# Reciprocal roots of the norms and of the last read-outs: ScalarE's logarithm and exponential with one Newton step, in place of an integer seed with three

## What is computed

```python
def rmsnorm(x, gain=None):
    xf = x.astype(jnp.float32)
    y = xf * lax.rsqrt(jnp.mean(xf * xf, axis=-1, keepdims=True) + EPS)
    ...

for l in range(DEPTH):
    hx = rmsnorm(x) * (1 + sc_a) + sh_a
    ...
    x = x + g_a * (jnp.concatenate([fx, ax, rx], axis=-1) @ w_out[l])
    x = x + g_f * swiglu(rmsnorm(x) * (1 + sc_f) + sh_f, w_gate[l], w_up[l], w_down[l])
return rmsnorm(x, final_norm)
```

## Time and profile before

| | |
|---|---|
| time, three runs | 1946.1 us median (1939.06, 1946.1, 1947.41) |
| span of the profiled execution | 1944.5 us |
| PE busy | 1773.0 us (91% of the span) |
| DVE busy | 1292.1 us (66%) |
| ACT busy | 839.4 us (43%), 12 loads of a table set among it |
| POOL busy | 83.8 us (4%) |
| DMA | 300.36 MB, mean 154 GB/s |

### The profile page before, as it was taken

The page is one execution under the profiler, slowest core; times in us unless marked ns, Lnnn a source line. Parts: engine busy times, 40 slices in busy tenths (PEclk is TensorE's granted clock), DMA queues, the critical chain, the costliest instruction groups (busy, mean ns, idle before and its releaser), DMA issues.

```text
span 1944.5 us, 30955 instructions
## 1 busy us (share of the span) xinstructions
PE 1773.0 (91%) x12242; PEld 1589.2 (82%) x12242; DVE 1292.1 (66%) x2365; ACT 839.4 (43%) x1661; POOL 83.8 (4%) x154
## 2 busy tenths in 40 slices
PE   4899988989999999898788999989899998989997
PEld 2788866888888888688678999777799987879996
DVE  1336678558878666557885788868678885675544
ACT  2523674252222222444653544366544435665432
POOL 1000124000000000001030000000000000000000
PEclk8889998899999999899787999989999998999999
DMA  8552111055546664234243899633399863416653
GB/s 252 184 190 87 33 45 45 6 150 170 173 162 204 186 189 160 85 111 114 84 135 84 255 263 281 237 120 78 109 264 274 274 228 113 127 44 174 184 175 130
DMA packets 359391, 300.36 MB, mean 154 GB/s; under 512 B 8320, under 2 KB 333680, under 8 KB 358992
## 3 DMA queue, kind: packets, MB, share of 16 engines
q1 hardware_dynamic: 357824, 294.22, 49.7%
q0 software_dynamic: 1424, 4.16, 0.9%
HBM read 297.30 MB, written 1.05 MB: 153 GB/s over the span
## 4 chain that ended last, share of the span: by engine, by line
PE 72%; DVE 11%; DMA 7%; ACT 5%; issue 4%; SPq 0%; DVEq 0%; POOL 0%; ACTq 0%; POOLq 0%
PE bank L958 70%; PE bank L972 2%; DMA raw<-in_w_up 2%; ACT whigh L1556 2%; DMA raw<-in_w_down 2%; DVE wlow L2057 1%; DVE ACC L2073 1%; DVE A L2430 1%; DMA A<-in_w_ada 1%; DMA raw<-in_ffn_w_out 1%; ACT A L1784 1%; DVE HTL L2182 1%; DMA X<-in_ctx 1%; DMA raw<-in_ffn_w_in 0%; DVE A L2174 0%
## 5 line engine op out<-in xcount | busy, mean ns | idle before, releaser
L2057 DVE TENSOR_TENSOR wlow<-raw,whigh 128x2048 fp32r<-128x2048 f32 (+1 forms) x183 | 409.8, 2243 | 301.5 <-ACT whigh L1556 301.0
L1556 ACT ACTIVATE whigh<-raw 128x2048 fp32r<-128x2048 f32 (+1 forms) x183 | 343.0, 1878 | 315.9 <-PE bank L958 99.1
L958 PE MATMUL bank<-HTH,whigh 128*128 128x256 f32 (+1 forms) x1424 | 444.4, 312 | 8.5 <-DVE HTL L2182 8.2
L958 PE MATMUL bank<-HTH,wlow 128*128 128x256 f32 (+1 forms) x1424 | 440.4, 309 | 0.0
L958 PE MATMUL bank<-HTL,whigh 128*128 128x256 f32 (+1 forms) x1424 | 440.2, 309 | 0.0
L958 PE MATMUL bank<-whigh,HTH 128*128 128x256 f32 (+1 forms) x1008 | 297.5, 295 | 23.0 <-DVE HTL L2300 6.3
L958 PE MATMUL bank<-wlow,HTH 128*128 128x256 f32 (+1 forms) x1008 | 293.1, 291 | 0.0
L958 PE MATMUL bank<-whigh,HTL 128*128 128x256 f32 (+1 forms) x1008 | 292.7, 290 | 0.0
L958 PEld LDWEIGHTS bank<-HTH,whigh 128*128 128x128 f32 x1424 | 273.6, 192 | 21.8 <-issue 8.9
L958 PEld LDWEIGHTS bank<-HTH,wlow 128*128 128x128 f32 x1424 | 273.4, 192 | 13.7
L958 PEld LDWEIGHTS bank<-HTL,whigh 128*128 128x128 f32 x1424 | 273.7, 192 | 12.6
(11 more groups left out here) (233 smaller groups left out, 2251.4 us busy)
## 6 DMA issues: line engine op xcount, KB each, us to landing
raw<-in_ffn_w_in SPq DMA_DIRECT2D x88, 512.0 KB, 5.4
A<-in_ada_w SPq DMA_DIRECT2D x38, 1024.0 KB, 7.4
A<-in_w_ada SPq DMA_DIRECT2D x32, 1024.0 KB, 5.5
raw<-in_w_gate SPq DMA_DIRECT2D x44, 512.0 KB, 6.6
raw<-in_w_up SPq DMA_DIRECT2D x44, 512.0 KB, 6.3
raw<-in_ffn_w_out SPq DMA_DIRECT2D x20, 1024.0 KB, 5.5
raw<-in_w_in SPq DMA_DIRECT2D x18, 1024.0 KB, 5.6
raw<-in_w_down SPq DMA_DIRECT2D x18, 1024.0 KB, 6.7
```

What stands on the lines that cost most here:

```text
L958: return nc.tensor.matmul(out, lhsT, rhs, start=start, stop=stop, skip_group_check=True)
L1556: nc.scalar.activation(parts(loads[n])[0], raw_slot(loads[n]), ACT.Copy).then_inc(*made("split_high", loads[n]))
L2057: V.tensor_tensor(low, raw_slot(loads[n]), as_float(high), ALU.subtract).then_inc(*made("split_low", loads[n]))
```

## The change

The integer guess and two of the three Newton steps are replaced, in ten places: the seven norms, the last norm, and the read-outs of tiles 0 and 1 in layers 0 and 1. There ScalarE computes Ln of the mean square and then Exp of minus half of it into `rs`, and VectorE, which meanwhile makes minus half the mean square, runs one Newton step on that (`polish`). In the norms ScalarE takes the mean inside the Ln: scale 1/D, and as bias the mean of the first half, column by column, one Ln per tile; then one Exp for all. These stand in ScalarE's list behind the squares of the second half and ahead of `norm_scaled(l, st, 0, 2, 3)`. In the norm before layer 2, and in the two read-outs, ScalarE waits for VectorE's mean square and runs one Ln and one Exp. `refine` stays for the first norm, the heads, the read-out of tiles 2 and 3, and `final_roots`. The preload of the set with Ln and Exp moves from the projections of layers 2 and 3 to the end of each layer's hidden features (behind `high(fs[-1])`, ahead of the down projection), in all four layers.

```diff
+            def root_seeds(l, st, tiles):
+                n = len(tiles)
+                if (l, st) == (2, "mix"):
+                    act.wait_ge(*upto("mean_square", l, st))
+                    last = nc.scalar.activation(logs[:, 0:n], ms[:, 0:n], ACT.Ln)
+                else:
+                    act.wait_ge(*upto("mean_half", l, st))
+                    for t in tiles:
+                        act.wait_ge(*upto("squared", l, st, 1, t))
+                        last = nc.scalar.activation(logs[:, t:t + 1], lsum[:, 1, t:t + 1], ACT.Ln, scale=1.0 / D, bias=ms[:, 8 + t:9 + t])
+                last.then_inc(*made("root_log", l, st))
+                act.wait_ge(*upto("root_log", l, st))
+                nc.scalar.activation(rs[:, 0:n], logs[:, 0:n], ACT.Exp, scale=-0.5).then_inc(*made("root_seed", l, st))
+
+            def head_seeds(l, t0, n):
+                act.wait_ge(*upto("mean_square", l, "scan", t0))
+                nc.scalar.activation(logs[:, 0:n], ms[:, 0:n], ACT.Ln).then_inc(*made("root_log", l, "scan"))
+                act.wait_ge(*upto("root_log", l, "scan"))
+                nc.scalar.activation(rs[:, 0:n], logs[:, 0:n], ACT.Exp, scale=-0.5).then_inc(*made("root_seed", l, "scan"))
...
             def norm(l, st):
                 tiles, more = tiles_of(l, st), len(pairs_of(l, st)) > 1
                 squares(l, st, tiles, lambda: norm_scaled(l, st, 0, 0, 1))
+                root_seeds(l, st, tiles)
                 norm_scaled(l, st, 0, 2, 3)
...
-                    if l >= 2 and at == 1:
-                        nc.scalar.preload_act_table_set("natural_log_exp_and_others")
...
                     high(fs[-1])
+                    if half == halves(l) - 1:
+                        nc.scalar.preload_act_table_set("natural_log_exp_and_others")
...
                         fourier_out(l, g)
+                        if g == 0:
+                            head_seeds(l, 0, 8)
...
                     squares(l, "final", X_TILES)
+                    root_seeds(l, "final", X_TILES)
...
+            def polish(l, st, n, done):
+                m, half, root, t = ms[:, 0:n], half_ms[:, 0:n], rs[:, 0:n], nw[:, 0:n]
+                link(V.tensor_scalar(half, m, -0.5, None, ALU.mult))
+                dve.wait_ge(*upto("root_seed", l, st))
+                link(V.tensor_tensor(t, root, root, ALU.mult))
+                link(V.tensor_tensor(t, t, half, ALU.mult))
+                V.scalar_tensor_tensor(out=root, in0=t, scalar=1.5, in1=root, op0=ALU.add, op1=ALU.mult).then_inc(*made(*done))
+
             def row_norms(l, st, tiles, done=None):
                 n = len(tiles)
+                if done:
+                    dve.wait_ge(*upto("squared", l, st, 0, tiles[-1]))
+                    V.tensor_scalar(ms[:, 8:8 + n], lsum[:, 0, 0:n], 1.0 / D, EPS, ALU.mult, ALU.add).then_inc(*made("mean_half", l, st))
+                    dve.wait_ge(*upto("squared", l, st, 1, tiles[-1]))
+                    dve.wait_ge(*upto("mean_half", l, st))
+                    link(V.scalar_tensor_tensor(out=ms[:, 0:n], in0=lsum[:, 1, 0:n], scalar=1.0 / D, in1=ms[:, 8:8 + n],
+                                                op0=ALU.mult, op1=ALU.add))
+                    polish(l, st, n, done)
+                    return
...
-                refine(2, "mix", n=2, done=("rooted", 2, "mix"))
+                dve.wait_ge(*upto("mean_square", 2, "mix"))
+                polish(2, "mix", 2, ("rooted", 2, "mix"))
...
-                refine(l, "scan", t0, n=4 * n)
+                if t0 == 0:
+                    dve.wait_ge(*upto("mean_square", l, "scan", t0))
+                    polish(l, "scan", 4 * n, ("rooted", l, "scan"))
+                    dve.wait_ge(*upto("rooted", l, "scan"))
+                else:
+                    refine(l, "scan", t0, n=4 * n)
```

More of the change, by code:

```diff
@@ L445, in block_kernel @@
         nw = sb("nw", [P, 16])
+        logs = sb("logs", [P, 8])
         nmax = sb("nmax", [P, 2, 4])
@@ L2701, in _ @@
                 if l == 3:
-                    row_norms(l, "final", X_TILES)
+                    row_norms(l, "final", X_TILES, ("rooted", l, "final"))
+                    dve.wait_ge(*upto("rooted", l, "final"))
                     dve.wait_ge(*upto("final_gain_in", l))
```

## The result

| kernel | median us | executions | profiled execution: time, span, clock |
|---|---|---|---|
| before | 1946.76 (1939.06 to 1949.46) | 4 | span 1944.5, clock 0.945 |
| after | 1929.38 (1926.24 to 1932.7) | 4 | 1932.7, span 1930.9, clock 0.956 |

The ratio after to before is 0.9919, with a 95% interval of 0.989 to 0.9947: 17.4 us between the medians, where 6.3 had been forecast and the range ended at 1932. The first question is how much of this lies at the roots.

A forecast was written before the change was run, and what follows sets the result against it. TensorE bounds the kernel, idle for the root chain in seven norms. 2 × 0.93 + 2 × 1.19 + 1.00 + 0.47 + 0.57 = 6.3 us; 1946.1 − 6.3 = 1939.8 us, range 1932 to 1946.

The forecast's parts named there:

- What bounds the kernel: At seven norms TensorE waits for the last Newton step; the whole root chain is on the path, the rest follows.
- The chain, term by term: Root chain in the norms: summed instruction times and hand-overs gave gains of 1.19 us with two tiles, 0.93 with four.
- T: In a norm, the end of the accumulator's last read; TensorE's spread started at T + 2.56 us before the change.
- Layer 2's mixing norm: Norm before layer 2, where ScalarE waits for VectorE's mean square: spread at 1283.59 in place of 1284.59, gain 1.00 us.
- These two norms give 0.47 and 0.57: Norms at 1073.68 and 1615.36: a 1.81 us gate row fills TensorE's time, capping gains at its idle 0.47 and 0.57.
- The hidden edits: Later ScalarE copies, the last norm, two read-outs and thirteen table loads in place of twelve: each 0 on the path.
- how the numbers follow: Closing step that set chances: 1939 to 1942 us 0.56, faster by over 0.5% 0.25, slower 0.04, within 0.71.
- the runs' own spread of 8 us: Spread of the kernel's run times, used with most of rival A and Rival B to set the range 1932 to 1946.
- rival A: Behind the norms: shorter stalls save TensorE stretches at half clock, 3 to 7 us more, 1933 to 1937; chance 0.22.
- if the clock's low stretches differ by more than two: A sign in the profile after that would make the prediction wrong: over two stretches of low clock more or fewer.
- Rival B: Feed-forward parts of layers 1 and 2: weight DMA waits absorb the gains up to layer 2, 1942.6 to 1944.3; chance 0.18.
- Rival C: In the norms: Ln or Exp from another table set brings two 1.28 us loads each, 1956.6 us; chance 0.04.

The follow-up runs named there:

- norms_only: The changed kernel with the two read-outs back on the integer guess and three Newton steps; median 1933.55 us, ratio to before 0.9969.
- pad_first12: The changed kernel with twelve extra dependent VectorE instructions in layer 0's feed-forward norm alone; median 1936.95 us, ratio to before 0.9968.
- pad_norms: The changed kernel with six extra dependent VectorE instructions in each of the seven norms; median 1938.45 us, ratio to before 1.0002.
- one_step: The kernel before with one Newton step instead of three behind the integer guess in the change's ten places; median 1930.67 us, ratio to before 0.9944.
- half_roots: The changed kernel with the squares of the second half of the columns left out in six norms; median 1922.71 us, ratio to before 0.9904.
- tables_in_norms: The changed kernel with the Ln and Exp table preload back in the projections of layers 2 and 3; median 1944.16 us, ratio to before 0.9987.
- pad_norms24: The changed kernel with 24 extra dependent VectorE instructions in each of the seven norms; median 1969.69 us, ratio to before 1.0144.
- after_third: The changed kernel run a third time, unaltered, in 11 executions; median 1938.74 us, ratio to before 0.9974.
- preload_only: The kernel before with only the Ln and Exp table preload moved to the end of the hidden features; median 1946.28 us, ratio to before 1.0029.
- before_early_gain: The kernel before with the final gain fetched early into the free half of its buffer; median 1942.37 us, ratio to before 1.0.
- early_gain: The changed kernel with the final gain fetched early into the free half of its buffer; median 1936.65 us, ratio to before 0.9953.

## Why the prediction was wrong

**What bounds the kernel: right.** Only TensorE's seven waits counted, and everything behind them followed at a fixed distance. Over the kernels, most of what the norms gain in the traces comes out in the time at equal clock: −7.0 and −7.0 (norms_only), −6.0 and −4.4 (pad_first12), +0.4 and −0.3 (pad_norms), −8.4 and −6.8 (one_step), −16.0 and −13.5 (half_roots), −7.6 and −6.4 ± 0.6 (the changed kernel, all executions). It does not for two: −0.35 and −3.5 (tables_in_norms), +27.5 and +15.6 (pad_norms24). There the plain means agree with the traces: −1.7 ± 1.7 and +27.2 ± 2.1 against before beside them.

**The chain, term by term: right in its mechanism.** Two tiles: spread at T + 1.31 where 1.37 was forecast, gain 1.25 for 1.19; the dependent start on ScalarE was 0.03 and not 0.09. Four tiles: T + 1.69 where 1.64 was forecast, because the Lns stand 0.19 apart and not 0.15. Layer 2's mixing norm: 1.11 for 1.00.

**"These two norms give 0.47 and 0.57": mis-sized.** Measured were 1.24, 1.25 and 0.60 for the first and 0.86, 1.25 and 1.02 for the second. The bound itself, the gate row that fills the time, is real: where that row ran at half clock, the first norm gave 0.60 (after_third) and 0.68 (norms_only). The row in after_third:

```profile
1071.77 1.91 PE L959 MATMUL bank<-ident,modc 128*128 128x128 f32 x8
```

But I took the row's 1.81 as fixed, and it is 1.06 at full clock. The sums came out 1.2, 1.6 and 1.1 us above 6.3, and these two norms make 1.1, 1.5 and 0.6 of that; in after_third another 0.5 is layer 2's mixing norm, whose gain was 1.49.

**The hidden edits: right.** The moved copies, the last norm (VectorE idle 2.54, forecast 2.4), the read-outs (norms_only, 7.0 without them) cost and gave nothing that can be told. Thirteen table loads, none in a norm. For the loads alone preload_only leaves room for about 1 us of loss.

**The step that failed is how the numbers follow, in two places.** First, the range: "the runs' own spread of 8 us" was read from three executions. The 86 executions of before that ran beside the experiments lie between 1930.4 and 1953.6, a spread of 23 us and not 8, with nine in ten between 1932.3 and 1951.3. Medians of four drawn from them lie between 1936.5 and 1949.2 in 95 of 100 cases, and of four drawn from the changed kernel's 21 between 1928.9 and 1941.5, below 1932 in one case of five. A range for the median of a few executions has to hold this beside the cases; mine ended at 1932. The median of all 21, 1935.7, lies inside the range: that the first four fell out of it was the luck of their clocks. Second, rival A and its condition "if the clock's low stretches differ by more than two" treated a differing clock as a consequence of the change. The low stretches differ by that much between two executions of the same kernel, with the same seven short stalls: layer 1's recurrence ran at full clock in after and at half clock in after_third.

**Where the 17.4 us went.** Over its 21 executions the changed kernel has a mean of 1935.3 ± 1.4 and a median of 1935.7; before has 1943.4 ± 0.6 over 86. That is 8.2 ± 1.5 us, 0.42%, of which 6.4 ± 0.6 stand at equal clock. The traces give 7.4 to 7.9 in the norms, and 0.4 us more lie outside the span: the time exceeds the span by 2.2 us in before, preload_only and before_early_gain and by 1.8 in all the others, for a reason that no run shows. The rest of the 17.4 was the draw of eight executions: the changed kernel's four had a mean of 1929.4 at a clock of 0.957, its other 17 a mean clock of 0.951, and the median of before's four stood 2.3 us above that of its 86. Against 0.5% the first comparison is a gain (0.25 was given to it), and all executions together are just short of one.

**Rival A** can't be excluded for a small part. The kernels with short roots and neither added stalls nor left-out squares (the changed kernel, norms_only, one_step, early_gain; 53 executions) have a mean clock of 0.9520 ± 0.0005, those with the old ones (before, preload_only, before_early_gain; 108 executions) 0.9507 ± 0.0003. By the slope that is 1.8 ± 0.9 us, below the rival's 3 to 7, though 3 is within two standard errors, and where it comes from is open: the 5.5 us in layer 1's recurrence, the largest single piece, came with long roots in pad_norms and stayed away with short ones in norms_only, early_gain and after_third. **Rival B** fails as priced: it left 1.8 to 3.5 us of gain, and there are 6.4 ± 0.6 at equal clock and 8.2 ± 1.5 in the means. **Rival C** does not occur, but the preload is what keeps it away.

## What to carry to other kernels

Before splitting a gain into causes, run both kernels often enough to see how far one kernel's own executions lie apart, and subtract traces matmul by matmul up to the first changed instruction: what differs there is no effect of the change. A short dependent chain that TensorE waits for is worth its length in full, and can be summed from rows; a bound that comes from work beside it must be priced at both levels of the clock. A comparison at equal clock serves while the stalls stay about as long as they were; where an edit makes them much longer, it left out part of the cost here, and the plain means did not. When two functions of ScalarE follow each other on the path, put the load of the set that holds both ahead of the stall: two loads cost more than the whole gain of a norm here.

## What the runs showed of the hardware

- Executions of one kernel (before, 86 of them), with identical instructions, had mean granted clocks between 0.944 and 0.959; over all kernels the times followed it by 13.8 us for 0.01.
- Without the set that holds both, an Ln and the Exp behind it brought a table load of 1.28 us each (tables_in_norms); the next ACTIVATE started 0.02 behind each load.
- A chain over two engines pays little at the hand-overs: 0.03 from one ScalarE instruction to the one that needs it, 0.11 from ScalarE to VectorE, 0.06 from VectorE to TensorE (1728.85 to 1728.91).
- Lns of 128x1 with their bias from memory stood 0.19 apart, for a single column each; four of them (0.84) were longer than four dependent VectorE instructions (0.78).
